# The first nine expert chunks of each mixture-of-experts stage, sent to other buffers

## The reference

```python
def _hier_moe(h, w_r1, b_r1, w_r2, b_r2, w_gate, w_up, w_down):
    t = h.reshape(b * n, d)
    logit_g = (t @ w_r1).astype(jnp.float32) + b_r1          # 4 groups
    grp = jnp.argmax(logit_g, axis=-1)
    ...
    top_v, top_i = lax.top_k(logit_e, MOE_TOPK)              # 2 of the group's 8 experts
    w_sel = jax.nn.softmax(top_v, axis=-1) * gate_g
    ...
    def expert_step(acc, xs):                                # over all 32 experts
        wg, wu, wd, gcol = xs
        y = (jax.nn.silu(t @ wg) * (t @ wu)) @ wd
        return acc + y.astype(jnp.float32) * gcol[:, None], None
```

## Time and profile before

| | |
|---|---|
| median of three runs | 2212.3 us (2211.49 to 2212.36) |
| the profiled execution's own time | 2211.73 us |
| its span | 2209.9 us |
| busy: TensorE matmuls, VectorE, ScalarE | 2117.2, 940.2, 566.5 us (96%, 43%, 26%) |
| bytes read from HBM | 618.59 MB, 280 GB/s over the span |
| SP queue's packets | 68.8% of the span of 16 DMA engines |
| chain that ended last | PE 75%, DMA 15%, DVE 7% |
| expert loads | 192 chunks of 2048 KB |

### The profile page before, as it was taken

The page is one execution under the profiler, slowest core; times in us unless marked ns, Lnnn a source line. Parts: engine busy times, 40 slices in busy tenths (PEclk is TensorE's granted clock), DMA queues, the critical chain, the costliest instruction groups (busy, mean ns, idle before and its releaser), DMA issues.

```text
span 2209.9 us, 31040 instructions
## 1 busy us (share of the span) xinstructions
PE 2117.2 (96%) x12934; PEld 1470.8 (67%) x12934; DVE 940.2 (43%) x1857; ACT 566.5 (26%) x1058; POOL 0.8 (0%) x6
## 2 busy tenths in 40 slices
PE   8999999999999999999988999999988999999987
PEld 7876779998877889998977544443335644443333
DVE  6898735542643345566365511211113512111112
ACT  2124123331135033344245311111112311111112
POOL 0000000000000000000000000000000000000000
PEclk9999999999999999999998999999999999999999
DMA  6445664546435654534240999999999699999995
GB/s 273 152 153 229 256 239 153 190 183 261 166 115 216 252 214 178 189 120 159 77 190 13 427 424 426 426 426 428 424 427 427 245 423 425 426 426 428 427 425 211
DMA packets 50079, 621.23 MB, mean 281 GB/s; under 512 B 5552, under 2 KB 5680, under 8 KB 12080
## 3 DMA queue, kind: packets, MB, share of 16 engines
q1 hardware_dynamic: 49824, 619.53, 68.8%
q10 hardware_dynamic: 144, 0.13, 0.0%
HBM read 618.59 MB, written 1.05 MB: 280 GB/s over the span
## 4 chain that ended last, share of the span: by engine, by line
PE 75%; DMA 15%; DVE 7%; ACT 1%; issue 1%; SPq 0%; ACTq 0%; DVEq 0%
PE bank L651 21%; DMA ring<-in_experts 12%; PE bank L1332 12%; PE bank L1355 7%; DMA arena<-in_experts 3%; PE sums L871 3%; PE sums L870 3%; PE sums L869 3%; PE bank L869 3%; PE bank L870 3%; PE bank L871 3%; PE sums L1365 2%; PE bank L1018 2%; PE bank L1020 2%; PE bank L1019 2%; DVE wide L2009 2%
## 5 line engine op out<-in xcount | busy, mean ns | idle before, releaser
L651 PE MATMUL bank<-h,ring 128*128 128x256 f32 x1568 | 345.7, 381 | 0.0
L651 PEld LDWEIGHTS bank<-h,ring 128*128 128x128 f32 x1568 | 297.1, 191 | 47.9 <-issue 6.5
L2241 DVE TENSOR_TENSOR ring_split<-ring,arena_split 128x2048 fp32r<-128x2048 f32 x64 | 144.2, 2289 | 150.7 <-ACT arena_split L1633 150.5
L2690 DVE TENSOR_TENSOR wide<-bank,wide 128x256 f32<-128x256 f32 x64 | 27.2, 425 | 385.3 <-ACT wide L1831 385.3
L2697 DVE SCALAR_TENSOR_TENSOR scratch_split<-bank,small,wide_split 128x512 fp32r<-128x512 f32 x64 | 48.1, 751 | 272.4 <-ACT wide_split L1839 272.4
L1633 ACT ACTIVATE arena_split<-ring 128x2048 fp32r<-128x2048 f32 x64 | 119.3, 1906 | 157.8 <-PE sums L871 144.1
L1332 PE MATMUL bank<-ring,h 128*64 128x512 f32 x640 | 143.7, 595 | 15.1 <-DMA ring<-in_experts 15.1
L1332 PE MATMUL bank<-arena,wide 128*64 128x512 f32 x608 | 137.0, 595 | 10.9 <-DMA arena<-in_experts 10.8
L869 PE MATMUL bank<-h_split,arena_split 128*128 128x256 f32 x512 | 145.8, 285 | 1.5 <-DVE scratch_split L2263 1.5
L869 PE MATMUL sums<-smax_split,arena_split 128*128 128x256 f32 x512 | 144.9, 283 | 0.0
L870 PE MATMUL sums<-smax_split,arena_split 128*128 128x256 f32 x512 | 144.9, 283 | 0.0
(11 more groups left out here) (387 smaller groups left out, 3600.1 us busy)
## 6 DMA issues: line engine op xcount, KB each, us to landing
ring<-in_stream SPq DMA_DIRECT2D x99, 2048.0 KB, 7.7
ring<-in_experts SPq DMA_DIRECT2D x96, 2048.0 KB, 29.4
arena<-in_experts SPq DMA_DIRECT2D x72, 2048.0 KB, 27.2
arena<-in_experts SPq DMA_DIRECT2D x22, 1024.0 KB, 23.9
stat<-in_experts SPq DMA_DIRECT2D x22, 512.0 KB, 24.8
scratch<-in_experts SPq DMA_DIRECT2D x22, 512.0 KB, 26.8
extra<-in_experts SPq DMA_DIRECT2D x2, 2048.0 KB, 26.8
arena<-in_stream SPq DMA_DIRECT2D x1, 2048.0 KB, 29.3
```

The lines of the kernel that those rows point to most:

```text
L651: mm = pe.matmul(dst, a, b, start=(first and i == 0), stop=(i == len(terms) - 1))
L2241: dve.tensor_tensor(split["ring"][:, slot, 2048 * part:2048 * part + 2048], v, HI[("up", "down")[part]][:, j % 2, :].bitcast(F32), ALU.sub ...
```

## The change

q0 to q8 go to other buffers. A tuple FIRST_SLOTS gives them: q0 to buffer 0, q1 to 1, q2 to 8, q3 to 6, q4 to 2, q5 to 3, q6 to 4, q7 to 5 and q8 to 7. The waits of layer 0's first nine loads go with the buffers and stand in a function of their own, freed_by_mixer, where buffer 6 now has a wait on the last neighbourhood-attention product (y, na, 3). In layer 1's stage the order of the buffers at the start is as it was, with other chunk numbers in them; the chunk in the last buffer, 7, is q8. From q9 on the buffers are taken as before, (q - 1) % 8, and each load waits for the chunk that lies there. That is q0 for q9 and q1 for q10 as before, and now q4 for q11, q5 for q12, q6 for q13, q7 for q14, q3 for q15 and q8 for q16. TensorE's order of work is the same; it reads the chunks from their new places.

```diff
+        FIRST_SLOTS = (0, 1, 8, 6, 2, 3, 4, 5, 7)
+
         def expert_slot(q, first):
 
             if first and q <= EXPERT_RING:
-                return q
+                return FIRST_SLOTS[q]
             return (q - 1) % EXPERT_RING
...
                 def first_slots():
 
                     sp.wait_ge(S.sem("moe0_down_done"), rounds_more[0] * EXPERTS + (EXPERTS - 3))
-                    load_expert_chunk(sp, S, i, 0, EXPERT_RING, first=True)
-                    for q in range(1, EXPERT_RING - 1):
-                        used(0, rounds_more[0] * TURN_PAIRS, EXPERTS * EXPERT_CHUNKS - EXPERT_RING + 1 + q)
-                        load_expert_chunk(sp, S, i, 0, q, first=True)
+                    load_expert_chunk(sp, S, i, 0, FIRST_SLOTS.index(EXPERT_RING), first=True)
+                    for slot in range(1, EXPERT_RING - 1):
+                        used(0, rounds_more[0] * TURN_PAIRS, EXPERTS * EXPERT_CHUNKS - EXPERT_RING + 1 + slot)
+                        load_expert_chunk(sp, S, i, 0, FIRST_SLOTS.index(slot), first=True)
                     S.wait(sp, "chunk_used", C_POOL)
                     load_expert_chunk(sp, S, i, 0, 0, first=True)
+                    S.wait(sp, "filled", "router", i)
+                    load_expert_chunk(sp, S, i, 0, EXPERT_RING, first=True)
+
+                def freed_by_mixer(q):
+
+                    slot = FIRST_SLOTS[q]
+                    if slot == 0:
+                        S.wait(sp, "filled", "ret", 1)
+                    elif slot == 1:
+                        sp.wait_ge(S.sem("ret_ready"), S.value("ret_ready", 0))
+                    elif slot == EXPERT_RING:
+                        S.wait(sp, "read", "s", "na", 15)
+                    elif slot == EXPERT_RING - 2:
+                        S.wait(sp, "filled", "y", "na", 3)
+                    elif slot == 2:
+                        S.wait(sp, "chunk_used", C_POOL - 1)
+                    elif slot == EXPERT_RING - 1:
+                        S.wait(sp, "filled", "router", i)
...
                     for q in range(PAIR_CHUNKS):
-                        if start and i and q <= EXPERT_RING and q != EXPERT_RING - 1:
-                            continue
...
-                        if first and EXPERT_RING < q <= 2 * EXPERT_RING:
-                            used(i, done, q - EXPERT_RING - 1)
-                        elif not start or q > EXPERT_RING:
+                        slot = expert_slot(q, first)
+                        if q <= EXPERT_RING and first:
+                            if start and i:
+                                continue
+                            if start:
+                                freed_by_mixer(q)
+                            elif slot < EXPERT_RING:
+                                used(i, done, slot - EXPERT_RING + 1 if slot < EXPERT_RING - 1 else -EXPERT_RING)
+                        elif first and q <= 2 * EXPERT_RING:
+                            used(i, done, FIRST_SLOTS.index(slot))
+                        else:
                             used(i, done, q - EXPERT_RING)
                         load_expert_chunk(sp, S, i, pair, q, first)
```

More of the change, by code:

```diff
@@ L1305, in landed @@
                         loads, a_round = 1, 1
-                    elif first and q < EXPERT_RING:
+                    elif first and q <= EXPERT_RING:
                         loads, a_round = 1, 3 * TURN_PAIRS - (slot == EXPERT_RING - 1)
```

## The result

The changed kernel takes 2224.8 us (median of 5 runs, 2221.95 to 2226.32) against 2212.3 us before; the ratio is 1.0056, 95% interval 1.0046 to 1.0067. The forecast was 2226.5 us in a range of 2221 to 2231. The profiled execution took 2224.77 us with a span of 2223.0, so the spans lie 13.1 us apart.

The account below looks back on a forecast made before the run. The prediction took the DMA stream of expert chunks to bound both expert stages. Delays of 6.8 us in the first and 7.4 us in the second, 14.2 us on 2212.3, gave 2226.5 us, range 2221 to 2231.

Parts of the forecast that it names:

- The bound: Both expert stages: DMA, 14.77 us per expert against TensorE's 13.20, sets the time; each stage ends when its chunk stream ends.
- Two loads earlier: Layer 0's stage: q2 and q3 go out by 1195, moving 9.84 us of transfer, but buying only 1.3 us by q10.
- q11's wait: First refills, both stages: q11 waits for q4 instead of q2, 6.87 us later in layer 0's, and blocks the loads behind.
- Layer 0's stage, 6.8 us: First expert stage: q13 starts at 1274.9 instead of 1268.1, a delay of 6.8 us, early loads already counted.
- Layer 1's stage, 7.4 us: Second expert stage: q13 starts at 1777.3 instead of 1769.9, a delay of 7.4 us, with no early loads.
- The sum: Whole kernel: the two stages' delays, 6.8 + 7.4 = 14.2 us, added to the time before, giving 2226.5 us.
- The restart of 1.6 us: DMA queue restarting from empty: the stream runs as if it began 1.6 us after the issue; bounds 0 and 2.8.
- The first wait: Expert stages: TensorE's first gate/up product waiting for a DMA comes some 4 experts, 55 us, earlier.
- A: Layer 0's stage: only bytes count, two early chunks shorten the stream by 9.84 us; 2202.5 us, chance 0.04.
- B: Both stages: the gaps vanish in TensorE's store of chunks; no change, 2212.3 us, chance 0.05.
- C: Expert stages: one stage pays and the other does not; 7 us, 2219.3 us, chance 0.07.
- D: Experts 3 or 4: late chunks make TensorE itself wait; a larger loss, over 2231 us, chance 0.04.

Follow-up runs that it names:

- e6: The kernel before, with each down chunk from the first refill on loaded by half; 2170.0 us.
- e7: The changed kernel, with each down chunk from the first refill on loaded by half; 2169.6 us.
- e3: The kernel before with its old buffers; only layer 0's first loads reordered so that two go out early; 2212.0 us, ratio 1.0002.
- e5: The kernel before with its places and load order; only q9 to q16 get the changed kernel's waits, both stages; 2224.8 us, ratio 1.0054.
- e1: The changed kernel with the new places in layer 0's stage only, the old ones in layer 1's; 2218.3 us, ratio 1.0033 to before.
- e2: The changed kernel with the new places in layer 1's stage only, the old ones in layer 0's; 2218.6 us, ratio 1.0033 to before.
- e4: The changed kernel with q15's load put ahead of q11's in each stage; 2218.6 us, ratio 1.0030 to before.
- e8: The changed kernel's places and early loads, but refills in TensorE's order of use, buffer 8 filled once more; 2211.1 us, ratio 0.9992 to before.

## Why the prediction was right, and where its sizes were off

- **The bound.** Right: each stage ends with its stream. e6 and e7 show it from the other side. But one number under it was misread. "45.5 us" of TensorE's waiting for chunks in a stage is a sum over two rows of one engine, the matmuls (16.3) and the weight loads (29.2), which partly lie beside each other. The view was asked for a line, and it adds both. For the same reason the forecast that this sum would rise by 7 us per stage is wrong: it went from 45.5 to 60.8 in layer 0's stage, by 5.8 on the matmuls' row and 9.5 on the weight loads'. The conclusion stood, since either row alone leaves more waiting than the 7 us.
- **Two loads earlier.** Their times were right (1186 and 1193), and also that they would not count by their bytes. The 1.3 us left to them did not enter the sum, since q13's start was reckoned from q12's issue, but they were expected of e3 and not found there. "The early loads have bought 1.3 us" holds only up to q10. The step that fails is to carry it further: the next refills wait for TensorE as well. "From here TensorE gives buffers back faster than the DMA fills them" does not hold for the first refill round, where it took 39.6 us for eight chunks against the DMA's 39.4.
- **q11's wait.** Right in place, cause and size: 6.87 us later, by the issues. e5 reproduces the whole loss by it alone.
- **Layer 0's stage, 6.8 us.** The landing is 6.6 us later (7.2 by the stream's length, with q9 issued 0.6 us earlier). e1 gives 6.8.
- **Layer 1's stage, 7.4 us.** 6.4 by the length, 7.1 in e2. This term was 1 us too large by the profiles. The old stream's thin stretch to 1790 (418 GB/s) came partly after 1769.9, the point from which I compared, so the old order was credited with a rate that it did not have; the new one, a hole late, is past that gate. By the rows this explains 20 x (1 - 418 / 426) = 0.4 us. Over the 42.15 us from q9's issue the two kernels moved 398 and 328 GB/s, which is a delay of 6.9 us; where the other 0.5 us to the landing go is open, and no more than single lengths scatter.
- **The sum.** 14.2 forecast, 13.7 by the lengths, 13.1 by the spans, 12.5 by the medians. The forecast lies 1.7 us above the median, within the spread of the runs (2221.95 to 2226.32). The restart of 1.6 us, taken from one row, held well enough: in the changed kernel q9 and q10 moved at 378 GB/s from 1755 to 1766, as if the stream had begun 1.8 us after q9's issue at 1754.46. By the 2 us of the Trainium skill's page "SBUF — State Buffer" (section "The DMA setup-cost knee") the forecast would, by this estimate, have been 0.8 us higher, further from what was measured; the trace's shorter time decides here.
- **The first wait.** Forecast 4 experts or 55 us earlier. In the kernel before, the first gate/up product that waits for a chunk is this one of the timeline (the bracket is the idle time before it and what ended it):

```profile
1482.98 0.20 PEld L1332 LDWEIGHTS bank<-arena,wide 128*64 128x64 f32 x4 [0.92 <-DMA arena<-in_experts]
```

In the changed kernel the idle time of the same line has no such row up to 1425 us, and up to 1430 this one, so the first wait came 53 to 58 us earlier:

```profile
  DMA ring<-in_experts: 0.7, 1
```

- **Rivals.** A fell with e3, B with the median, C with e1 and e2, where both stages pay. D would have needed waits of TensorE for a chunk before 1300; neither its gate/up nor its down products have one.

## What to carry to other kernels

Where buffers are filled by one queue in order, the order in which they come free and the order in which they are filled again belong together: a permutation of the first fill changes who each refill waits for, and the in-order queue makes the latest of them everybody's wait. Loads moved into an idle stretch were worth nothing here (e3), since the store behind them was full anyway; look for the first refill and ask what releases it, then for the second. An engine that is 100% busy in the stretch where the time is lost is no evidence that nothing is lost there, if a later stretch of it waits for the same stream; a pair of runs in which the stream is made light (e6, e7) tells at once.

## What the runs showed of the hardware

A stream restarted from an empty queue ran as if it began 1.6 us after its issue (4.06 MB in the 11 us to 1759.0), 1.8 us in the changed kernel. In the 28 us after e4's hole, where each refill went out when TensorE had freed its buffer, the stream moved 410 and 400 GB/s instead of 426; why is not shown. In e8's profiled execution, the 16 matmuls after the last landing of layer 0's stage took 5.38 us in the chain, and 3.68 in the kernel before. Its windows show why; the column before the last two is the granted clock:

```profile
1672.00:1676.00 4.00, 2.02 (x10) 0.48 (x8) 0.00 (x0) 0.00 (x0) 0.00 (x0) 1.00 1.00 418
1676.00:1678.00 2.00, 2.00 (x10) 0.70 (x8) 0.00 (x0) 0.00 (x0) 0.00 (x0) 0.69 1.02 434
1678.00:1680.00 2.00, 2.00 (x8) 0.56 (x6) 0.00 (x0) 0.00 (x0) 0.00 (x0) 0.50 1.02 434
```

After waiting about half of the 4 us to 1676 TensorE was granted 0.50 of its clock, 1.2 instead of 2.4 GHz, for the last products, at a cost of 1.7 us on the path. The kernel before waits there as well (TensorE is busy 2.76 of the same 4 us) and kept 1.00 in its profile. So a stage that waits for its stream lost a little more than the wait in this execution; why in this one and not in the others is open.
